# A hybrid SSD and sparse-attention layer: the compressed scores in two places, three groups of the norm moved to later units

## What is computed

```
h = rmsnorm(x, g_pre) * (1 + scale) + shift
z, xbc, dt, q, kv, nsa_gate, z_att, merge_gate = split(h @ w_in)
# Mamba-2 branch: norm over 4 groups of 512 channels, then the output product
y = ssd(conv(xbc), dt) * silu(z)
y_ssm = rmsnorm(y.reshape(256, 4, 512), g) @ w_ssm_out
# compressed attention: 15 blocks of keys and values, 16 heads
kc = silu(blocks(k) @ w1_k) @ w2_k          # the same for v
sc = q . kc * scale - slope * distance      # compressed scores, 256 x 16 heads x 15
p_c = softmax(sc);  o_cmp = p_c @ vc
o = g0 * o_cmp + g1 * o_slc + g2 * o_win
y_nsa = (o * silu(z_att)) @ w_nsa_out
merged = sig(mg0) * y_ssm + sig(mg1) * y_nsa
out = x + gate * rmsnorm(merged @ w_out, g_post)
```

## Time and profile before

| | us |
|---|---|
| Time, median of 3 runs | 454.94 (454.66 to 456.67) |
| The profiled execution, its own time | 455.79 |
| Its span, from the first to the last instruction | 454.0 |
| TensorE busy in the span | 435.1 (96%) |
| VectorE busy | 346.3 (76%) |
| ScalarE busy | 281.5 (62%) |
| GpSimd busy | 205.6 (45%) |

### The profile page before, as it was taken

The page is one execution under the profiler, slowest core; times in us unless marked ns, Lnnn a source line. Parts: engine busy times, 40 slices in busy tenths (PEclk is TensorE's granted clock), DMA queues, the critical chain, the costliest instruction groups (busy, mean ns, idle before and its releaser), DMA issues.

```text
span 454.0 us, 9851 instructions
## 1 busy us (share of the span) xinstructions
PE 435.1 (96%) x3638; PEld 400.5 (88%) x3638; DVE 346.3 (76%) x615; ACT 281.5 (62%) x560; POOL 205.6 (45%) x195
## 2 busy tenths in 40 slices
PE   2899999999999999999899999999999999999995
PEld 2597999999999999986899999999989899999873
DVE  0366889999999999468788879478668888787633
ACT  3245885878687986656898647476557554544441
POOL 0147661533346436735483444355443653355430
PEclk9999999999999999999999969999999999999999
DMA  7999636474535436168756442424344364497002
GB/s 283 420 415 397 210 135 186 139 232 141 171 110 167 158 141 184 49 198 274 266 190 214 160 140 95 139 93 152 129 160 165 140 244 176 170 385 249 33 0 92
DMA packets 22391, 84.04 MB, mean 185 GB/s; under 512 B 2492, under 2 KB 2882, under 8 KB 21186
## 3 DMA queue, kind: packets, MB, share of 16 engines
q1 hardware_dynamic: 22344, 83.42, 52.6%
HBM read 82.36 MB, written 1.05 MB: 184 GB/s over the span
## 4 chain that ended last, share of the span: by engine, by line
PE 50%; DVE 1%; issue 0%; ACT 0%; DVEq 0%
PE gemm L727 12%; PE gemm L729 11%; PE gemm L728 11%; PE y_or_o L933 3%; PE score L897 1%; PE score L899 1%; PE small L871 1%; PE score L900 1%; PE small L652 1%; PE small L654 1%; PE score L654 1%; PE score L653 1%; PE small L653 1%; PE score L652 1%; PE small L909 1%; PE small L915 1%
## 5 line engine op out<-in xcount | busy, mean ns | idle before, releaser
L1574 POOL TENSOR_TENSOR w_lo<-w_raw,w_hi 128x256 fp32r<-128x256 f32 x89 | 116.0, 1307 | 159.1 <-ACT w_hi L955 150.6
L727 PE MATMUL gemm<-h_hi,w_hi 128*128 128x256 f32 x600 | 171.5, 286 | 2.1 <-DVE cmp_hidden L1300 1.2
L729 PE MATMUL gemm<-h_hi,w_lo 128*128 128x256 f32 x600 | 167.8, 280 | 0.0
L728 PE MATMUL gemm<-h_lo,w_hi 128*128 128x256 f32 x600 | 167.8, 280 | 0.0
L1230 DVE TENSOR_TENSOR w_lo<-w_raw,w_hi 128x768 fp32r<-128x768 f32 (+1 forms) x117 | 128.1, 1098 | 42.8 <-ACT w_hi L955 42.3
L955 ACT CAST w_hi<-w_raw 128x1024 fp32r<-128x1024 f32 x117 | 122.2, 1045 | 44.8 <-PE gemm L729 25.2
L727 PEld LDWEIGHTS gemm<-h_hi,w_hi 128*128 128x128 f32 x600 | 114.1, 190 | 5.9 <-issue 3.0
L728 PEld LDWEIGHTS gemm<-h_lo,w_hi 128*128 128x128 f32 x600 | 114.3, 191 | 0.8 <-issue 0.2
L729 PEld LDWEIGHTS gemm<-h_hi,w_lo 128*128 128x128 f32 x600 | 113.9, 190 | 0.0
L727 PE MATMUL gemm<-ynorm_hi,w_hi 128*128 128x256 f32 x128 | 36.1, 282 | 0.0
L729 PE MATMUL gemm<-ynorm_hi,w_lo 128*128 128x256 f32 x128 | 35.4, 276 | 0.0
(11 more groups left out here) (253 smaller groups left out, 893.0 us busy)
## 6 DMA issues: line engine op xcount, KB each, us to landing
w_raw<-in_wpack SPq DMA_DIRECT2D x133, 512.0 KB, 3.7
w_ada_shift_scale<-in_w_ada SPq DMA_DIRECT2D x8, 1024.0 KB, 15.5
x_T<-in_xT SPq DMA_DIRECT2D x2, 512.0 KB, 5.9
x_residual<-in_x_tok SPq DMA_DIRECT2D x1, 1024.0 KB, 6.1
out_tok_dram<-out_tok SPq DMA_DIRECT2D x4, 256.0 KB, 2.1
ada_gate_products<-in_gate_bias SPq DMA_DIRECT2D x1, 512.0 KB, 4.0
g_post_rows<-in_g_post_rows SPq DMA_DIRECT2D x1, 512.0 KB, 5.7
consts<-in_consts SPq DMA_DIRECT2D x1, 272.0 KB, 22.0
```

What stands on the lines that cost most here:

```text
L727: nc.tensor.matmul(bank[:, 0:SEQ], w_hi, hi[:, k0 + k, :], start=first, stop=False)
L728: nc.tensor.matmul(bank[:, 0:SEQ], w_hi, lo[:, k0 + k, :], start=False, stop=False)
L729: last = nc.tensor.matmul(bank[:, 0:SEQ], w_lo, hi[:, k0 + k, :], start=False, stop=end)
L1574: nc.gpsimd.tensor_tensor(WL[:, n % LO_SLOTS, c:1024], RAW[:, u % RAW_SLOTS, c:1024], WH[:, n % HI_SLOTS, c:1024], ALU.subtract).then_inc( ...
```

## The change

Two things are moved in the written order, and two follow from it.

- Step "cs" i no longer takes all heads of a query half, but the heads 8i to 8i + 7 of both halves. "cs" 0 stands behind unit q6 and "cs" 1 behind vw0, each with sixteen products. VectorE's additions come in eight instructions of half the size. "cs" 0 waits for the read-out of q0 to q3, "cs" 1 for that of q4 to q7.
- Of the later norm, group 0 stays in the w1k stage. The reciprocal of group 1 goes from behind w1k2 to behind vs0, and its tiles 4 to 7 from the w1v, kw and vs units to vs0, vs1, q1 and q3. The reciprocal of group 2 goes from vs0 to mg1, that of group 3 from vs1 to mg7, and their tiles 8 to 15, of which four were in the vs and q units, all to mg2 to mg14 (mg2, 4, 5, 6, 8, 9, 10, 12; the last roundings up to mg14).
- rstd_y01 gets a place of its own at the end of the memory, since it lives on into the q units.

```
-    norm_units = [w1k + 1, w1k + 2, w1k + 4, w1k + 5, w1v + 1, w1v + 2, w1v + 4, ks + 2, ks + 4, q + 1, q + 3, q + 5]
-    norm_units += [mg + n for n in (4, 6, 8, 10, 12, 14)]
-    for g, u in enumerate((w1k + 1, w1k + 3, ks + 4, ks + 5)):
+    norm_units = [w1k + 1, w1k + 2, w1k + 4, w1k + 5, ks + 4, ks + 5, q + 1, q + 3]
+    norm_units += [mg + n for n in (2, 4, 5, 6, 8, 9, 10, 12, 13, 14)]
+    for g, u in enumerate((w1k + 1, ks + 4, mg + 1, mg + 7)):
...
-    after_tile(q7 + 1, ("cs", 0), ("cs", 1))
+    after_tile(q7 - 1, ("cs", 0))
+    after_tile(q7 + 1, ("cs", 1))
...
-    RN = [place("rstd_y01", [P, 2, SEQ], f32, at=q_at + 32 * kb), place("rstd_y23", [P, 2, SEQ], f32, at=ag_at + 2 * kb)]
+    RN = [place("rstd_y01", [P, 2, SEQ], f32, at=over_at + 50 * kb), place("rstd_y23", [P, 2, SEQ], f32, at=ag_at + 2 * kb)]
...
-                    for j in (6, 7):
+                    for j in range(4 * i, 4 * i + 4):
                         wait_tile_out(pe, ("q", j))
...
-                    for h in range(ATT_HEADS):
-                        last = nc.tensor.matmul(bank[:, 32 * h:32 * h + 32], QS[:, h, P * i:P * i + P], KC[:, h // HPG, :],
-                                                start=True, stop=True)
+                    for t in range(2):
+                        for h in range(8 * i, 8 * i + 8):
+                            o = 256 * t + 32 * (h % 8)
+                            last = nc.tensor.matmul(bank[:, o:o + 32], QS[:, h, P * t:P * t + P], KC[:, h // HPG, :],
+                                                    start=True, stop=True)
...
-                    sc = bank[:, :].rearrange("p (h n j) -> p h n j", h=ATT_HEADS, n=2)
-                    bias = CBI[:, 0:512].rearrange("p (t h j) -> p t h j", t=2, h=ATT_HEADS)[:, i]
-                    link(nc.vector.tensor_tensor(CSW[:, i], sc[:, :, 1, :], bias, ALU.add))
-                    nc.vector.tensor_tensor(CSW[:, i], sc[:, :, 0, :], CSW[:, i], ALU.add).then_inc(release, 1)
+                    sc = bank[:, :].rearrange("p (t h n j) -> p t h n j", t=2, h=8, n=2)
+                    bias = CBI[:, 0:512].rearrange("p (t h j) -> p t h j", t=2, h=ATT_HEADS)
+                    for t in range(2):
+                        scores = CSW[:, t, 8 * i:8 * i + 8, :]
+                        link(nc.vector.tensor_tensor(scores, sc[:, t, :, 1, :], bias[:, t, 8 * i:8 * i + 8], ALU.add))
+                        last = nc.vector.tensor_tensor(scores, sc[:, t, :, 0, :], scores, ALU.add)
+                    last.then_inc(release, 1)
```

More of the change, by code:

```diff
@@ L331, in build @@
     kb = 1024
-    assert over_at + 50 * kb <= 229344, over_at
+    assert over_at + 52 * kb <= 229344, over_at
     ADA = place("w_ada_shift_scale", [P, 2, KT, 1024], f32, at=z_at)
```

## The result

| | before | after |
|---|---|---|
| Median of 20 runs each, same chip (us) | 455.10 (454.27 to 456.92) | 457.09 (455.01 to 459.00) |
| Ratio after/before | | 1.0037, 95% interval 1.0027 to 1.0048 |
| The profiled execution (us) | 455.79 | 456.28 |
| Its span (us) | 454.0 | 454.5 |

The changed kernel is slower, by 0.37%. (The ratio is not that of the two medians, which lie 2.0 us apart and would give 1.0044.) Forecast were 451.5 us and a range of 449.6 to 454.0; the time is above it. It lies within the 0.5% of "no change", and nowhere near the gain of 3.8 us that the sum gave.

The account below looks back on a forecast made before the run. TensorE, busy 96% of the span, was taken to bound the kernel through its work, stops and clock. Terms -3.2 - 1.9 + 0.1 (narrow-to-wide switch) + 1.2 = -3.8 gave 452.0 or 451.1, so 451.5 us; range 449.6 to 454.0.

Parts of the forecast that it names:

- The stage: Compression stage: without the norm there, TensorE's stops of 0.7 and 1.2 us for cmp_hidden go, -1.9 us (1.0 to 1.9).
- The clock: At the 32 narrow compressed-score products: split into two sixteens, the clock no longer falls, -3.2 us (bounds -3.2 to +3.2).
- The additions: VectorE's part of the compressed scores: eight half-size additions take 2.5 us in all; cost 0, up to 1.3 without cover.
- The merge gates: Moved norm work, about 9.3 us of VectorE, arrives there; TensorE's stops cost +1.2 us (bounds 0 to 4.2).
- The stops at the scores: Merge gates: TensorE's scores wait for ScalarE's exponentials, 0.5 us from reciprocal 2 and 0.7 from a y_tmp and ynorm_lo pair.
- VectorE takes the gain back: Rival, merge gates: moved tiles pile up, 3.0 us of stops, and the stage gives only 1.0; 453.8 to 454.7 us; chance 0.14.
- The rival on the slower side: Rival: the clock falls at both blocks of sixteen, some 13 us at 1.2 GHz, 457.9 us; chance 0.05.

Follow-up runs that it names:

- the norm alone: The kernel before with only the norm's lines and the place of rstd_y01 changed, compressed scores left in one place: 454.76 us, ratio 0.9995.
- the copy moved: The kernel before with only head 1's copy of the second half of the transposed probabilities moved from VectorE to ScalarE: 454.37 us, ratio 0.9984.
- the scores alone: The kernel before with only the compressed scores split into two places, the norm left where it was: 455.16 us, ratio 1.0006.
- the reciprocal alone: The changed kernel with the reciprocal of group 2 behind vs1 instead of mg1, its tiles left in the merge gates: 454.05 us, ratio 0.9982.
- "ct" later: The changed kernel with the transposes of the compressed probabilities one unit later, behind mg3 instead of mg2: 456.67 us, ratio 1.0032.
- "both": The changed kernel with the reciprocal of group 2 behind vs1 and head 1's second probability copy on ScalarE instead of VectorE: 453.52 us, ratio 0.9952.
- the scores alone with the copy moved: The kernel before with only the compressed scores split into two places and head 1's second probability copy on ScalarE: 454.25 us, ratio 0.9977.
- the norm alone with the copy moved: The kernel before with only the norm's move and head 1's second probability copy on ScalarE: 453.46 us, ratio 0.9953.

## Why the prediction was wrong

**The stage: right.** Predicted -1.9, measured -2.2 at the matmul of 218.7 us, 0.8 and 1.4 of it for the two stops of 0.7 and 1.2. No new bound came from the weights: the transfers' share rose from 0.81 and 0.83 to 0.84 and 0.88 and no engine waited longer.

**The clock: the mechanism right, its worth wrong.** Narrow products, not a pause, made it fall: 32 in a row brought a fall in each of the four profiled executions that have them (before, the norm alone, and both with the copy moved), sixteen and sixteen brought none at the products in the eight. The 3.2 us did arrive (-5.5 at 271.8). What was mis-sized is the term's worth in the whole. Executions of before without a fall are only 0.9 to 1.3 us faster than those with a whole one, and the median lies 0.2 to 0.3 above them. I had written that I couldn't see how much of the loss the median has; it has a tenth of the 3.2. The prediction took each us that TensorE saves for a us of the whole, and didn't ask whether TensorE would have waited a little later anyway.

By the Trainium skill, "TensorE: Matmul & The Clock Gate", section "HAM oscillation — how this bites in real kernels", pauses between bursts bring such falls. The old fall had none ahead of it. The new one, at 281.7 us, has: it came during the 3.2 us of standstill, and there the trace agrees with the page. Shorter ones, of 1.7 us (the scores alone, the reciprocal alone) and 2.4 us ("ct" later), weren't followed by a fall in their profiled executions.

**The additions: right.** Eight of 0.28 to 0.29 us, 2.3 in all (said 2.5), and no wait came from them.

**The merge gates: the step that failed.** This term of the sum was put at 1.2 us and measured 6.0, the 5.0 + 1.0 that the table shows lost: 3.2 at "ct", some 1.4 at half clock behind it, 0.3 at v's transposes, 0.9 at the scores. The prediction says that queued behind the new steps are the maxima, with them the exponentials and the scores, and that the next late thing would be the transposes of probabilities "a us behind". It followed one chain from VectorE to TensorE. There is a second through the same queue: behind the maxima comes the copy that gives a bank back to "ct", and it comes first for TensorE. Its reserve could be read in before: copy ended at 283.17, fifth transpose at 284.19. With my own shifts (TensorE 1.9 + 3.2 sooner, VectorE some 0.8 sooner and 1.75 later again) the same three rows give 5.1 + 0.95 - 1.0 = 5.0 us of waiting, if VectorE's start isn't drawn along with TensorE's; measured were 3.2, since it was (3.0 us sooner). Already the 3.2 would have turned the sum round: -3.8 + 3.2 + 1.4 for the half clock behind it = +0.8 on the profiled execution; measured +0.5.

**The stops at the scores: nearly right in size, wrong in place.** Said were 0.5 behind mg3 and 0.7 behind mg7; measured 0, 0.45 and a later one of 0.4. Why the first didn't come is not shown; that the wait in "ct" lets VectorE and ScalarE catch up would fit. With that wait out of the way, in "both", the scores behind mg7 and mg11 lose 0.5 each against the scores alone with the copy moved, near the 1.2 that was said.

**The range.** Stops from 0 to 3 and a stage of 1.0 to 1.9 give, by the terms of the prediction, 449.9 to 454.7 from the two bases, and not 449.8 to 453.5; the measured time is above either.

**The rivals.** "VectorE takes the gain back" (453.8 to 454.7) was nearest in kind and too mild. It had the engine right, but as a pile-up over the whole of the gates; what happened was one instruction of 1.74 us ahead of one copy of 0.41. The rival on the slower side, falls at both blocks, didn't happen. The one that did was missing: slower through a standstill, with a fall of the clock behind it.

**What stays open.** The account above is that of two executions, 0.5 us apart; the medians are 2.0 apart. Of the other 1.5, before gives 0.7: its profiled execution has the whole fall and lies that much above its median. The profiled execution of after, 456.28 us, is 0.8 below the median of its runs; what the others lose more isn't seen in it (those with a lower mean clock are slower: 456.3 at 0.998, 457.2 at 0.994 to 0.996, and 459.0 and 457.5 for the two at 0.991 and 0.992). Open as well is what holds up the norm alone with the copy moved when its clock doesn't fall.

## What to carry to other kernels

When work is put into an engine's queue, follow every thing that stands behind it, not only the next chain: a copy that gives a buffer back counts as much as a result, and its reserve is read in two rows of before (end of the copy, start of its next user). Gains that come one after the other on the same engine run into the same later wait: first ask what that wait's reserve is (here 1.0 us), for more than that is saved only when the wait is shortened too. Here the norm's move alone, with one copy of 0.4 us on another engine, gives 453.46 us, 0.47% below before; the split of the products isn't needed for it.

## What the runs showed of the hardware that was not expected

- TensorE's clock went to half while TensorE counted as busy throughout, behind 32 products of 32 columns in a row; with twelve of 256 columns in their middle (1.3 us) it did not, nor in two blocks of sixteen. By the mean clocks, 32 in a row don't bring a fall in every execution.
- A fall of 6.8 us cost 3.2 us with the copy moved and 0.9 to 1.3 us without, where TensorE, had it come sooner, would have waited 12 us behind the fall's end.
- The length of a fall varies between executions of like kernels: 6.8 us in before and in the two with 32 in a row and the copy moved, 3.4 us with the norm alone, and 3.4 us behind the standstill in after.
